# A router that works on blocks without 1/rms, and constants and position biases loaded in another order

## The chip, the cores and the metric

The kernel runs on one core of one Trainium2 chip. The metric is the time of one execution on the device in microseconds (us), the median of several runs. The program is one launch and computes everything in fp32. Its engines are TensorE (PE in the profile, with its weight loads PEld), VectorE (DVE), ScalarE (ACT), GpSimd (POOL) and SyncE (SP); each has its own stream of instructions, and they meet at semaphores.

## What is computed

Two blocks of a transformer follow one another on 256 tokens of width 1024. The change lies in the first. Cut to what matters:

```python
mod = jax.nn.silu(c) @ w_ada[l] + b_ada[l]                 # shifts, scales and gates, 6 x 1024
sh1, sc1, gt1, sh2, sc2, gt2 = jnp.split(mod[:, None, :], 6, axis=-1)
h = rms_norm(x, g_pre_mix[l]) * (1.0 + sc1) + sh1
proj = h @ w_in[l]                                         # 1024 x 3072
...                                                        # 4 differential heads, 8 neighbourhood heads
bias = rpb.astype(jnp.float32)[:, dr[:, None, :, None], dc[None, :, None, :]]   # position biases
mix = jnp.concatenate([o_diff, o_nat], axis=-1) @ w_out[l]
x = x + gt1 * rms_norm(mix, g_post_mix[l])
h2 = rms_norm(x, g_pre_ffn[l]) * (1.0 + sc2) + sh2
logits = (hf @ w_router + b_router).astype(jnp.float32)    # hf is h2, 256 x 1024; 32 experts
top_val, top_idx = lax.top_k(logits, TOP_K)                # 4 of 32, gates by softmax
...                                                        # each token through its 4 experts
```

## The kernel before

**Start.** SP loads `x` (L384), 8 chunks of `w_ada` and 12 chunks of `w_in` (L381, L373). ACT loads `c` (L1231), then the constants `early_sb` (L1232: identity, ones, masks, epsilons), then 14 small vectors. POOL waits for the eighth chunk of `w_ada`, then loads the distance biases (`alibi`, L450, 1 MB) and the neighbourhood biases (L460: 32 transfers of 64 x 4 rows of 64 numbers, 256 bytes each), then router weights and other small things. PE runs `turn_c` (L488), `turn_x` (L502), the chunks of `w_ada` (`ada`, L521) with `vector_columns` (L492 to L495, turning the small vectors) after the second and the squares' sum `sum_squares(0, q)` (L539) after the fourth, then `ada_columns(0)` (L531) and the twelve chunks of `w_in` (`win_half`, L642). DVE waits first for the turned vectors (L1589 to L1601), then makes 1/rms (L1559), multiplies x by it (L1616), copies the `w_ada` sum (L1606) and scales `hT`.

**Middle.** Attention is woven into 24 half chunks ("slots") of `w_in` and 4 slots of the other 16 chunks of `w_ada`. From slot 8 on PE flips one head's biases in each slot (`flip_bias`, L625), and DVE adds the window.

**Router.** After `w_out` (L562), ACT and DVE make 1/rms of its result (L1218, L1559), and `onto_x` (L1576, L1578) adds to x, a quarter at a time. ACT squares each quarter (L1209), PE sums the squares over all 128 partitions (L539), ACT takes the root, DVE the reciprocal (L1559), DVE multiplies x by it (L1698, 8 tiles), ACT scales and shifts into `hT` (L1304, 8 tiles). Then PE makes the logits (L707, L709 for the bias row) and turns `hT` into token rows (L713). DVE picks the top four (L1704 to L1714), PE counts ranks (L718 to L722), DVE lists the jobs (L1728 to L1741), PE turns the list (L725), then adds b2 (L735), gathers token columns for the first pair of experts (L741), and the expert loop begins (L776, then L805; the first 12 chunks of expert weights are loaded by then). The loop ran 34 jobs in the profiled execution. In it ACT copies the next pair's gathered columns out of PSUM with one instruction a job (`save_half`, L1318).

## Time and profile before

| | us |
|---|---|
| runs | 2051.84, 2049.17, 2051.05 |
| median | 2051.05 |
| profiled execution | 2057.52 |
| its span in the trace | 2055.7 |
| PE busy in the span | 1961.8 (95%) |
| mean granted share of TensorE's clock | 0.984 |

Times in the trace count from the start of the span. A line such as "PE ... x64" merges 64 instructions, with what they wrote and read; in brackets stands the idle time of the engine ahead of them and what ended it. The granted clock is 1.00 (2.4 GHz) or 0.50 (1.2 GHz); a number between is a mean over a stretch.

### The profile page before, as it was taken

How to read it: one execution, taken by the hardware profiler on the slowest of the kernel's cores; microseconds unless marked ns; L12 is line 12 of the kernel's file. 1: busy time of each engine (PE TensorE's matmuls, PEld its weight loads, DVE VectorE, ACT ScalarE, POOL GpSimd, SP SyncE). 2: the span in 40 equal slices, each digit the busy share in tenths (PEclk: the TensorE clock that was granted, in tenths of full speed). 3: DMA queues.
4: the chain of work that ended last, by engine and by line, in shares of the span. 5: the costliest groups of instructions: out<-in, count | busy, mean ns of one | idle time of the engine just before them, and what ended most of it. 6: DMA issues, size and time to landing. Idle time of an engine off the chain costs nothing.

```text
span 2055.7 us, 25409 instructions
## 1 busy us (share of the span) xinstructions
PE 1961.8 (95%) x10105; PEld 1256.3 (61%) x10106; DVE 461.2 (22%) x880; ACT 315.4 (15%) x585; POOL 28.3 (1%) x49
## 2 busy tenths in 40 slices
PE   6999699999999999999999989999999999999998
PEld 4776544433334444443333338788888899888887
DVE  1432411101111111111011113441010277410101
ACT  1232211101111111111011112431000120210001
POOL 4000000000000000000000000000000000000000
PEclk9999699999999999999999998999999999999999
DMA  9939199999997979999999996334444433344410
GB/s 325 306 105 401 62 393 421 422 422 422 422 422 315 422 317 423 422 422 422 422 421 422 422 383 212 103 103 143 151 157 146 143 121 103 124 143 146 162 41 21
DMA packets 170248, 562.81 MB, mean 274 GB/s; under 512 B 10726, under 2 KB 110216, under 8 KB 117712
## 3 DMA queue, kind: packets, MB, share of 16 engines
q1 hardware_dynamic: 167504, 554.83, 69.8%
q0 software_dynamic: 1920, 6.29, 1.1%
q8 instruction: 44, 0.72, 0.1%
q10 hardware_dynamic: 768, 0.87, 0.1%
q14 instruction: 12, 0.10, 0.0%
HBM read 560.91 MB, written 1.05 MB: 273 GB/s over the span
## 4 chain that ended last, share of the span: by engine, by line
PE 72%; DMA 20%; SPq 4%; DVE 1%; issue 1%; ACT 0%; DVEq 0%; ACTq 0%
DMA ring<-in_w_dram 18%; PE psum L1069 15%; PE psum L776 12%; PE psum L805 7%; PE psum L1041 7%; PE psum L1102 5%; PE psum L848 5%; SPq L401 3%; PE psum L642 3%; PE psum L562 3%; PE psum L741 2%; PE psum L757 2%; DMA ring<-in_w_in_dram 1%; PE psum L1123 1%; PE psum L539 1%
## 5 line engine op out<-in xcount | busy, mean ns | idle before, releaser
L776 PE MATMUL psum<-ring,arena 128*64 128x512 f32 x2176 | 491.4, 596 | 43.3 <-DMA ring<-in_w_dram 41.4
L776 PEld LDWEIGHTS psum<-ring,arena 128*64 128x64 f32 x2176 | 152.1, 137 | 376.2 <-issue 253.0
L1069 PE MATMUL psum<-hT,ring 128*128 128x256 f32 x1408 | 307.5, 379 | 0.0
L1069 PEld LDWEIGHTS psum<-hT,ring 128*128 128x128 f32 x1408 | 267.5, 190 | 36.4
L805 PE MATMUL psum<-ring,arena 128*64 128x512 f32 x1088 | 241.0, 595 | 3.3
L1798 DVE TENSOR_SCALAR arena<-psum 128x512 f32<-128x512 f32 x34 | 23.5, 692 | 736.8 <-PE psum L783 736.8
L805 PEld LDWEIGHTS psum<-ring,arena 128*64 128x64 f32 x1088 | 77.7, 137 | 144.7 <-issue 144.7
L1041 PE MATMUL psum<-arena,ring 128*128 128x256 f32 x640 | 141.4, 379 | 0.0
L1041 PEld LDWEIGHTS psum<-arena,ring 128*128 128x128 f32 x640 | 121.6, 190 | 16.5
L1329 ACT ACTIVATE arena<-arena 128x512 f32<-128x512 f32 x34 | 21.4, 630 | 515.4 <-DVE arena L1798 515.4
L741 PE MATMUL psum<-arena 128*128 128x128 f32 x576 | 81.0, 286 | 0.0
L1102 PE MATMUL psum<-hT,ring 128*128 128x256 f32 x352 | 79.1, 379 | 0.0
L741 PEld LDWEIGHTS psum<-arena 128*128 128x128 f32 x576 | 71.4, 196 | 11.9 <-issue 11.9
L1492 ACT ACTIVATE arena<-arena 128x512 f32<-128x512 f32 x22 | 13.9, 630 | 394.5 <-DVE arena L1939 394.5
L1102 PEld LDWEIGHTS psum<-hT,ring 128*128 128x128 f32 x352 | 65.8, 190 | 10.1 <-issue 1.9
L757 PEld LDWEIGHTS psum<-arena 64*128 64x128 f32 x560 | 51.2, 186 | 33.8 <-issue 27.6
L757 PE MATMUL psum<-arena 64*128 64x256 f32 x560 | 69.9, 389 | 0.7 <-ACT arena L1339 0.7
L1939 DVE TENSOR_TENSOR arena<-psum,rstd 128x512 f32<-128x512 f32 x22 | 15.2, 692 | 238.3 <-PE psum L1069 238.3
L848 PE MATMUL psum<-hT,ring 128*128 128x256 f32 x288 | 66.3, 384 | 0.0
L562 PE MATMUL psum<-mixT,ring 128*128 128x256 f32 x288 | 63.7, 379 | 0.0
L642 PE MATMUL psum<-hT,ring 128*128 128x256 f32 x256 | 60.1, 392 | 0.5 <-DVE hT L1622 0.5
L848 PEld LDWEIGHTS psum<-hT,ring 128*128 128x128 f32 x288 | 53.9, 191 | 9.3 <-issue 2.4
(346 smaller groups left out, 1602.8 us busy)
## 6 DMA issues: line engine op xcount, KB each, us to landing
ring<-in_w_dram SPq DMA_DIRECT2D x384, 1024.0 KB, 23.2
ring<-in_ffn_w_dram SPq DMA_DIRECT2D x66, 1024.0 KB, 5.2
ring<-in_w_ada_dram SPq DMA_DIRECT2D x24, 1024.0 KB, 10.8
ring<-in_odd_w_in_dram SPq DMA_DIRECT2D x16, 1024.0 KB, 5.4
ring<-in_even_w_in_dram SPq DMA_DIRECT2D x13, 1024.0 KB, 12.4
ring<-in_w_in_dram SPq DMA_DIRECT2D x12, 1024.0 KB, 14.2
ring<-in_w_out_dram SPq DMA_DIRECT2D x4, 1024.0 KB, 15.5
ring<-in_even_w_out_dram SPq DMA_DIRECT2D x4, 1024.0 KB, 5.1
```

What stands on the lines that cost most here:

```text
L401: sp.dma_start(home[:, :], src).then_inc(landed[(C_MOE + j) % RING], 16)
L562: mm = nc.tensor.matmul(home[:, at:at + n_out], lhs, rhs, start=(k == 0), stop=(k == KT - 1))
L642: mm = nc.tensor.matmul(home, lhs, rhs, start=(k == 0), stop=(k == KT - 1))
L741: nc.tensor.matmul(home[:, (k % 4) * P:(k % 4 + 1) * P], h_tok[:, a, k * P:(k + 1) * P], pick[:, a, :], start=(a == 0), stop=(a == TT - 1))
L757: mm = nc.tensor.matmul(bank[k // 2][:, (k % 2) * T:(k % 2 + 1) * T], y_sb[half, t * P:(t + 1) * P], st_sb[r][half, :], start=False, stop= ...
L776: mm = nc.tensor.matmul(bank[4 + q][64 * h:64 * h + 64, :], xg[:, k, SLOTS * r:SLOTS * (r + 1)], ring[(C_MOE + k) % RING][:, (2 * h + q) * ...
L805: mm = nc.tensor.matmul(bank[7][64 * h:64 * h + 64, :], act_T[:, at:at + 64], w[:, k, 512 * h:512 * h + 512], start=(f == 0), stop=(f == 7))
L848: mm = nc.tensor.matmul(home[:, at:at + n_out], lhs, rhs, start=(k == 0), stop=(k == KT - 1))
L1041: mm = nc.tensor.matmul(bank[j // 2][:, (j % 2) * T:(j % 2 + 1) * T], w[:, k, j * P:(j + 1) * P], ffn_h[i % 2][:, k, :], start=(i == 0 and ...
L1069: mm = nc.tensor.matmul(bank[4 + 2 * (i % 2) + b][:, h * T:(h + 1) * T], cols(n)[:, k, h * P:(h + 1) * P], hT[:, k * T:(k + 1) * T], start ...
L1102: mm = nc.tensor.matmul(home, lhs, rhs, start=(k == 0), stop=(k == KT - 1))
L1798: V.tensor_scalar(glu, both[:, :, 0], LIMIT, None, ALU.min).then_inc(S.glu_ready, 1)
```

## The change

Five edits.

1. **Constants.** `early_sb` is laid out anew. SP loads its first 258 columns (identity, ones, epsilons) ahead of `x`, with a semaphore of their own (`ident_loaded`); ACT loads the rest behind the 14 small vectors. PE waits for `early_loaded` only at the first flip, DVE at the first window.
2. **Position biases.** 16 transfers of 64 x 6 rows of 256 bytes instead of 32 of 64 x 4 rows. Each half of the partitions keeps six rows of windows, of which the two blocks of queries use overlapping four, so a flip is two matmuls of 256 columns instead of one of 512. POOL issues them when the third chunk of `w_in` has landed.
3. **Order on PE at the start.** The squares' sum after the second chunk of `w_ada`, the turned vectors after the sixth.
4. **Router.** logits = (x\*g)@w / rms + (shift@w + b). The row in brackets is made during `w_out` (8 matmuls of one column, one that spreads it). ACT scales x by the gain alone into `hT`, without waiting for 1/rms. PE takes each quarter as it comes (`routed_part`): column sums of the squares (`ones[:, 0:1]`, one output column), logits, and the turn into token rows. 1/rms is a number for each token (`tok_rstd`), applied by DVE to the logits and by ACT to the token rows.
5. **Gathered columns.** They now lack the shift, so `save_half` adds it: four instructions of 128 columns with a bias instead of one of 512 in each job; ahead of the loop ACT does one half and DVE the other.

```diff
-N_EARLY = _columns(EARLY, [("ident", P), ("ones", P), ("before", P), ("flip", P), ("slot", 2 * SLOTS), ("eps", 2),
+N_EARLY = _columns(EARLY, [("ident", P), ("ones", P), ("eps", 2), ("before", P), ("flip", P), ("slot", 2 * SLOTS),
...
+            first_part = EARLY["before"][0]
+            sp.dma_start(early_sb[:, 0:first_part], early[:, 0:first_part]).then_inc(S.ident_loaded, 16)
             sp.dma_start(x_tok, x[0].rearrange("(a p) d -> p a d", p=P)).then_inc(S.x_loaded, 16)
...
-            for r in range(GRID_ROWS):
-                half = 64 * (r % 2)
+            pool.wait_ge(landed[(C_WIN + 2) % RING], 16)
+            for half in range(2):
                 for h in range(8):
-                    src = bass.AP(nat_rpb.tensor, h * 465 + (NAT_KH - 1 - r) * 31 + NAT_KW - 1 - (GRID_W - 1),
-                                  [[1, GRID_W], [31, GRID_ROWS], [1, GRID_W]])
...
+                    src = bass.AP(nat_rpb.tensor, h * 465 + (NAT_KH - 3 - half) * 31 + NAT_KW - 1 - (GRID_W - 1),
+                                  [[1, GRID_W], [31, NAT_WINDOWS], [1, GRID_W]])
...
-            vector_columns()
-            for n in range(2, 4):
-                ada(n)
             for q in range(4):
                 sum_squares(0, q)
-            for n in range(4, N_ADA_A):
+            for n in range(2, 6):
+                ada(n)
+            vector_columns()
+            for n in range(6, N_ADA_A):
                 ada(n)
...
+                if j == 1:
+                    pe.wait_ge(S.mod_ready, 1)
+                    pe.wait_ge(S.moe_loaded, 16 * 5)
+                    for k in range(KT):
+                        mm = nc.tensor.matmul(bank[7][0:1, 0:E_N], mod[:, 24 + k:25 + k], router_w[:, k, :],
+                                              start=(k == 0), stop=(k == KT - 1))
+                    mm.then_inc(S.shift_turned, 1)
...
+            def routed_part(q):
+                pe.wait_ge(S.sq_ready, 4 * 2 + q + 1)
+                for k in (2 * q, 2 * q + 1):
+                    for a in range(TT):
+                        sums = nc.tensor.matmul(bank[5][:, a:a + 1], sq[:, k * T + a * P:k * T + (a + 1) * P], ones[:, 0:1],
...
+                for k in (2 * q, 2 * q + 1):
+                    pe.wait_ge(S.h_ready, KT + k + 1)
+                    for a in range(TT):
+                        block = hT[:, k * T + a * P:k * T + (a + 1) * P]
+                        mm = nc.tensor.matmul(bank[4][:, a * E_N:(a + 1) * E_N], block, router_w[:, k, :],
...
-            squares(xT, S.x_ready, 4)
-            root(2)
-            for k in range(KT):
-                act.wait_ge(S.spread, k + 1)
-                nc.scalar.activation(hT[:, k * T:(k + 1) * T], sq[:, k * T:(k + 1) * T], ACT.Identity,
-                                     bias=mod[:, 24 + k:25 + k], scale=pre_scale[:, 8 + k:9 + k]).then_inc(S.h_ready, 1)
-
+            for q in range(4):
+                act.wait_ge(S.x_ready, 4 + q + 1)
+                square(xT, q)
+                for k in (2 * q, 2 * q + 1):
+                    nc.scalar.activation(hT[:, k * T:(k + 1) * T], xT[:, k * T:(k + 1) * T], ACT.Copy,
+                                         scale=pre_scale[:, 8 + k:9 + k]).then_inc(S.h_ready, 1)
...
-            def save_half(home, dst):
-                nc.scalar.activation(dst, home.rearrange("p (k s) -> p k s", s=2 * SLOTS), ACT.Copy).then_inc(S.half_saved, 1)
+            def save_half(r, home, dst):
+                for k in range(4):
+                    ins = nc.scalar.activation(dst[:, k, :], home[:, k * P:(k + 1) * P], ACT.Identity,
+                                               bias=mod[:, 24 + 4 * r + k:25 + 4 * r + k])
+                ins.then_inc(S.half_saved, 1)
...
-            inverse(2)
-            for k in range(KT):
-                V.tensor_tensor(sq[:, k * T:(k + 1) * T], xT[:, k * T:(k + 1) * T], rstd[:, :], ALU.mult) \
-                 .then_inc(S.spread, 1)
```

The order of PE's matmuls at the start, before: `turn_c`, `turn_x`, then chunks of `w_ada` (written to 32 x 512), turned vectors, squares' sum (128x256), `ada_columns`, and the first chunks of `w_in`.

```order
L488 MATMUL psum<-early_sb,arena 128x8
L502 MATMUL psum<-early_sb,arena 128x128 x16
L521 MATMUL psum<-ring,small 32x512 x8
L492 MATMUL psum<-early_sb,arena 128x128
L493 MATMUL psum<-early_sb,arena 128x2
L495 MATMUL psum<-early_sb,arena 128x32 x2
L521 MATMUL psum<-ring,small 32x512 x8
L539 MATMUL psum<-sq,early_sb 128x256 x8
L521 MATMUL psum<-ring,small 32x512 x16
L531 MATMUL psum<-early_sb,arena 128x4 x4
L509 MATMUL psum<-small,early_sb 128x2
L642 MATMUL psum<-hT,ring 128x256 x32
```

And now:

```order
L492 MATMUL psum<-early_sb,arena 128x8
L506 MATMUL psum<-early_sb,arena 128x128 x16
L525 MATMUL psum<-ring,small 32x512 x8
L543 MATMUL psum<-sq,early_sb 128x256 x8
L525 MATMUL psum<-ring,small 32x512 x16
L496 MATMUL psum<-early_sb,arena 128x128
L497 MATMUL psum<-early_sb,arena 128x2
L499 MATMUL psum<-early_sb,arena 128x32 x2
L525 MATMUL psum<-ring,small 32x512 x8
L535 MATMUL psum<-early_sb,arena 128x4 x4
L513 MATMUL psum<-small,early_sb 128x2
L650 MATMUL psum<-hT,ring 128x256 x32
```

The sum of squares has moved up by one pair of chunks and the three rows of turned vectors down by four chunks.

PE from the third chunk of `w_out` (128x256 into `psum` from `mixT,ring`) to the counting of ranks, before:

```order
L562 MATMUL psum<-mixT,ring 128x256 x16
L539 MATMUL psum<-sq,early_sb 128x256 x12
L707 MATMUL psum<-arena,hT 128x32 x8
L709 MATMUL psum<-arena,early_sb 128x32
L707 MATMUL psum<-arena,hT 128x32 x8
L709 MATMUL psum<-arena,early_sb 128x32
L713 MATMUL psum<-early_sb,hT 128x128 x16
L718 MATMUL psum<-arena,early_sb 128x32
```

And now, from the matmuls of the shift on; the three rows of a quarter repeat four times:

```order
L710 MATMUL psum<-arena,small 1x32 x8
L566 MATMUL psum<-mixT,ring 128x256 x16
L543 MATMUL psum<-sq,early_sb 128x256 x2
L715 MATMUL psum<-arena,early_sb 128x32
L566 MATMUL psum<-mixT,ring 128x256 x16
L543 MATMUL psum<-sq,early_sb 128x256 x4
L723 MATMUL psum<-early_sb,sq 128x1 x4
L731 MATMUL psum<-arena,hT 128x32 x4
L737 MATMUL psum<-early_sb,hT 128x128 x4
L723 MATMUL psum<-early_sb,sq 128x1 x4
L731 MATMUL psum<-arena,hT 128x32 x4
L737 MATMUL psum<-early_sb,hT 128x128 x4
L723 MATMUL psum<-early_sb,sq 128x1 x4
```

The sums over 256 columns are gone, the logits and turns stand in quarters behind sums of one column, and eight matmuls of one row (`1x32`) and one that spreads it stand between the chunks of `w_out`.

ACT in the same place, from the last square of the `w_out` result on, before:

```order
L1209 ACTIVATE sq<-hT 128x512
L1218 ACT_TABLE_LOAD
L1218 ACTIVATE rstd<-psum,early_sb 128x256
L1209 ACTIVATE sq<-xT 128x512 x4
L1218 ACTIVATE rstd<-psum,early_sb 128x256
L1304 ACTIVATE hT<-sq,small 128x256 x8
L1310 ACT_TABLE_LOAD
L1310 ACTIVATE arena<-arena 128x32 x2
L1314 ACTIVATE arena<-psum 128x1024 x2
```

And now:

```order
L1237 ACTIVATE sq<-hT 128x512
L1246 ACT_TABLE_LOAD
L1246 ACTIVATE rstd<-psum,early_sb 128x256
L1237 ACTIVATE sq<-xT 128x512
L1333 ACTIVATE hT<-xT,small 128x256 x2
L1237 ACTIVATE sq<-xT 128x512
L1333 ACTIVATE hT<-xT,small 128x256 x2
L1237 ACTIVATE sq<-xT 128x512
```

The second root is no longer ahead of the copies into `hT`; each quarter's two copies follow its square.

## Rows read from the trace of the kernel before

**Rows 1.** The page, part 4: share of the span by line in the chain.
```profile
DMA ring<-in_w_dram 18%; PE psum L1069 15%; PE psum L776 12%; PE psum L805 7%; PE psum L1041 7%; PE psum L1102 5%; PE psum L848 5%; SPq L401 3%; PE psum L642 3%; PE psum L562 3%; PE psum L741 2%; PE psum L757 2%; DMA ring<-in_w_in_dram 1%; PE psum L1123 1%; PE psum L539 1%
```
**Rows 2.** The chain in order of time, first 420 us: start us, us, what.
```profile
83.68 3.45 PE psum L642 x16
...
398.28 26.88 DMA ring<-in_w_dram
```
**Rows 3.** Timeline of the start: start us, us, engine, line, instructions [idle before <-releaser].
```profile
20.26 0.47 PE L492 MATMUL psum<-early_sb,arena 128*128 128x128 f32 x1 [4.69 <-DMA arena<-in_cmp_pos_v_dram]
...
27.83 3.64 PE L521 MATMUL psum<-ring,small 128*32 128x512 f32 x32
...
33.30 1.41 PE L531 MATMUL psum<-early_sb,arena 128*128 128x4 f32 x8 [1.83 <-DVE arena L1606]
...
35.72 16.49 PE L642 MATMUL psum<-hT,ring 128*128 128x256 f32 x64 [0.50 <-DVE hT L1622]
...
54.47 8.77 PE L642 MATMUL psum<-ring,hT 128*128 128x256 f32 x32 [2.25 <-DMA ring<-in_w_in_dram]
```
**Rows 4.** The same timeline, DVE alone, from 20 to 36 us.
```profile
21.22 0.28 DVE L1589 COPY small<-psum 128x120 f32<-128x120 f32 x1 [20.10 <-PE psum L495]
...
22.26 0.07 DVE L1601 DVE_READ_ACCUMULATOR2_ANT small<- 1x1 f32 x1
28.44 1.75 DVE L1559 RECIPROCAL rstd<-rstd 128x256 f32<-128x256 f32 x1 [6.11 <-ACT rstd L1218]
30.23 2.29 DVE L1616 TENSOR_TENSOR sq<-xT,rstd 128x2048 f32<-128x2048 f32 x1
32.56 0.69 DVE L1606 COPY arena<-psum 128x512 f32<-128x512 f32 x1
```
**Rows 5.** The same timeline, POOL's transfers of the biases.
```profile
28.01 0.56 POOL L450 DMA_DIRECT2D early_sb<-in_early_dram  x1 [24.65 <-DMA ring<-in_w_ada_dram]
...
28.56 19.56 POOL L460 DMA_DIRECT2D arena<-in_nat_rpb_dram  x32
```
**Rows 6.** Stretches: us, busy us (instructions) by engine, PEclk, DMA share, GB/s.
```profile
36.00:54.00 18.00, 16.21 (x64) 13.52 (x63) 2.03 (x8) 1.20 (x2) 15.11 (x25) 0.87 1.08 217
58.00:78.00 20.00, 19.57 (x98) 16.09 (x97) 7.68 (x12) 5.47 (x18) 0.00 (x0) 1.00 1.10 349
211.00:214.60 3.60, 3.60 (x9) 2.84 (x10) 3.53 (x8) 1.26 (x2) 0.00 (x0) 0.50 0.58 244
223.50:235.20 11.70, 11.66 (x52) 11.41 (x53) 2.30 (x16) 1.82 (x3) 0.00 (x0) 0.50 0.00 0
262.00:396.00 134.00, 133.51 (x718) 56.42 (x716) 19.96 (x38) 17.09 (x29) 0.00 (x0) 1.00 1.01 420
```
**Rows 7.** Timeline of the router, 195 to 260 us.
```profile
210.97 5.69 PE L539 MATMUL psum<-sq,early_sb 128*128 128x256 f32 x16 [4.82 <-ACT sq L1209]
...
219.44 4.04 ACT L1304 ACTIVATE hT<-sq,small 128x256 f32<-128x256 f32 x8 [2.28 <-DVE sq L1698]
...
223.53 3.62 PE L707 MATMUL psum<-arena,hT 128*128 128x32 f32 x16 [6.88 <-ACT hT L1304]
...
231.88 0.21 DVE L1704 COPY arena<-psum 128x64 f32<-128x64 f32 x1 [10.13 <-issue]
...
233.14 0.20 DVE L1714 TENSOR_SCALAR arena<-arena 128x64 f32<-128x64 f32 x1
...
235.02 0.41 PEld L718 LDWEIGHTS psum<-arena,early_sb 128*128 128x128 f32 x2
...
236.51 0.18 DVE L1728 TENSOR_SCALAR arena<-psum 128x32 f32<-128x32 f32 x1 [2.00 <-issue]
...
256.14 4.08 PE L776 MATMUL psum<-ring,arena 128*64 128x512 f32 x18 [1.83 <-ACT small L1349]
```
**Rows 8.** A group of ACT in the expert loop, 262 to 396 us: count, busy us, mean ns.
```profile
L1318 ACT ACTIVATE arena<-psum 128x512 f32<-128x512 f32 x5 | 3.0, 597 | 0.3
```
**Rows 9.** Timeline of the expert loop, PE: second matrices of one job.
```profile
647.05 7.09 PE L805 MATMUL psum<-ring,arena 128*64 128x512 f32 x32
```

More of the change, by code:

```diff
@@ L621, in flip_bias @@
                 if h == 0:
-                    pe.wait_ge(S.bias_loaded, 16 * 32)
+                    pe.wait_ge(S.early_loaded, 16)
+                if h == 0:
+                    pe.wait_ge(S.bias_loaded, 16 * 16)
                 if h >= 2:
                     pe.wait_ge(S.bias_ready, h - 1)
-                nc.tensor.matmul(bank[(5, 7)[h % 2]], flip, nat_bias[:, h, :], start=True, stop=True) \
-                  .then_inc(S.bias_flipped, 1)
+                for n in range(2):
+                    mm = nc.tensor.matmul(bank[(5, 7)[h % 2]][:, n * T:(n + 1) * T], flip,
+                                          nat_bias[:, h, P * (1 - n):P * (1 - n) + T], start=True, stop=True)
+                mm.then_inc(S.bias_flipped, 1)
             def win_half(i, half):
@@ L710, in _ @@
-            mm.then_inc(S.logits_ready, 1)
-            for a in range(TT):
-                for k in range(KT):
-                    mm = nc.tensor.transpose(bank[2 * a + k // 4][:, (k % 4) * P:(k % 4 + 1) * P],
-                                             hT[:, k * T + a * P:k * T + (a + 1) * P], ident)
+                if j == 1:
[5 more added lines that the diff above has]
+                    mm.then_inc(S.shift_turned, 1)
@@ new lines, in _ @@
+                if j == 2:
+                    pe.wait_ge(S.shift_row_ready, 1)
+                    nc.tensor.matmul(bank[7][:, 64:64 + E_N], ones[0:1, :], shift_row, start=True, stop=True) \
+                      .then_inc(S.shift_spread, 1)
+            sum_squares(1, 3)
+            def routed_part(q):
[3 more added lines that the diff above has]
+                        sums = nc.tensor.matmul(bank[5][:, a:a + 1], sq[:, k * T + a * P:k * T + (a + 1) * P], ones[:, 0:1],
+                                                start=(k == 0 and a == 0), stop=(k == KT - 1), skip_group_check=True)
+                if q == 3:
+                    sums.then_inc(S.ssq_ready, 1)
+                for k in (2 * q, 2 * q + 1):
[3 more added lines that the diff above has]
+                        mm = nc.tensor.matmul(bank[4][:, a * E_N:(a + 1) * E_N], block, router_w[:, k, :],
+                                              start=(k == 0 and a == 0), stop=(k == KT - 1), skip_group_check=True)
+                if q == 3:
+                    mm.then_inc(S.logits_ready, 1)
+                for k in (2 * q, 2 * q + 1):
+                    for a in range(TT):
+                        mm = nc.tensor.transpose(bank[2 * a + k // 4][:, (k % 4) * P:(k % 4 + 1) * P],
+                                                 hT[:, k * T + a * P:k * T + (a + 1) * P], ident)
+                return mm
@@ L1243, in _ @@
                     act.dma_start(pos_rows[i][:, 64 * g:64 * g + 64], v[0]).then_inc(S.vec_loaded, 16)
+            act.dma_start(early_sb[:, EARLY["before"][0]:EARLY["alibi"][0]], early[:, EARLY["before"][0]:EARLY["alibi"][0]]) \
+               .then_inc(S.early_loaded, 16)
             act.wait_ge(S.c_cleared, 1)
@@ L1344, in _ @@
             act.wait_ge(S.gathered, 1)
-            for r in range(2):
-                save_half(bank[6 + r], xg[:, 4 * r:4 * r + 4, :])
+            save_half(0, bank[6], xg[:, 0:4, :])
             save_gates(0, bank[5])
```

50 lines of the change are left out of this document (31 added, 19 removed).

## The prediction

> **What bounds the kernel now.** First the page's list of the chain by line: 18% is waiting for expert weights, nearly all the rest is PE [rows 1]. The chain in order of time shows the pattern: PE's steps follow one another without a gap until PE waits 26.88 us for expert weights, from 398.28 us on [rows 2]. From 262 to 396 us the DMA engines already move 420 GB/s with PE busy 133.5 of 134 us [rows 6], so in the expert loop the stream of weights is the limit. That stream starts when PE has used up its first chunk, in the row that begins at 256.14 us [rows 7]. What moves this row moves the stream, the loop and all behind it by as much; so the question is when that row begins. Two stretches ahead of it hold idle time that a reader can see.
>
> The first is the start. PE turns the small vectors at 20.26 us, after 4.69 us of waiting. It is done with the last chunk of `w_ada` at 31.47 us, though POOL's wait shows this chunk landed at 28.01 us [rows 3, 5]. DVE is the later one: 1/rms and the product occupy it from 28.44 to 32.52 us, and only then it copies the `w_ada` sum [rows 4]. The chunks of `w_in` begin at 35.72 us; the third of them is waited for 2.25 us, and the row behind that wait is slow, 8.77 us for what takes 2 x 3.45 at full clock [rows 2, 3].
>
> The second is the router: one step after another on ACT, PE and DVE, with PE at a granted clock of 0.50 from 223.5 to 235.2 us [rows 6, 7].
>
> **The start, edits 1 to 3.** The last chunk of `w_ada` is bound by the transfers: the bytes ahead of it stay nearly the same, so it still lands near 28.0 us. PE then takes 0.9 us for it (3.64 / 4), or 1.8 at half clock, and ends at 28.9 to 29.8. But DVE's program begins with the turned vectors, and these now come after the sixth chunk. That one lands two chunks of 2.5 us (1 MB at 420 GB/s) ahead of the last, at 23.0. PE needs 0.9 to 1.8 us for it and 1.0 to turn the vectors (20.26 to 21.22), so DVE starts at 24.9 to 25.8. It needs 1.1 us for the small work, 1.8 for 1/rms and 2.3 for the product [rows 3, 4], and copies the sum at 30.1 to 31.0, not at 32.56. DVE stays the later one. From that copy to the first matmul of `w_in` it took 3.16 us; if PE is at half clock all the while, its eight instructions there (1.41 us, partly at full clock) take some 0.4 more. I take the first matmul at 33.4, a gain of 2.3 us (1.2 to 3.0). The earlier identity and x gain nothing by themselves, since the chunks cover them.
>
> Now the wait for the third chunk. From 36 to 54 us the engines of the DMA were fully busy but moved 217 GB/s, against 349 from 58 to 78 us [rows 6]. So 3.9 MB went through in 18 us, of which 2.1 MB were biases in pieces of 256 bytes. The other 1.8 MB need 5.2 us at 349 GB/s, which leaves 12.8 us for the biases. With 1.57 MB instead it is 9.6 us. They now stand behind the third chunk: three chunks and the 1 MB of `alibi` are 4.2 MB, 12.0 us, all landed by 40.0. The second chunk is wanted at 33.4 + 6.9 + 2.5 (half clock at first, as before) = 42.8, the third at 49.7, the fourth at 56.6. Even if every bias went ahead of the fourth chunk, that one would land at 40.0 + 9.6 + 3.0 = 52.6. So the wait goes, and with it the slow row behind it: 2.25 us and 8.77 - 6.90 = 1.87 us. Next late would be the biases themselves at the first flip, which comes after four chunks, later than 61 us. POOL issues 16 transfers in 10 us (0.61 each [rows 5]), up to 50. Before, it had issued the last at 48.1 us and the third chunk, clogged by them, was in at 54.5; allowing the same 6.4 us they are there by 57. The split flips stream the same columns. Between the first slots and the router PE has no idle worth naming, so the 6.4 us (2.3 + 2.25 + 1.87) are kept. Bounds: 4.8 (late start, half clock a little longer) to 9 (first chunks at full clock).
>
> **The shift's row, edit 4.** Eight matmuls of one column and one that spreads the row are 18 instructions on PE in the midst of `w_out`, where PE has no gap: a cost. The nearest row is the logits, 16 instructions in 3.62 us at half clock, 0.226 each [rows 7], so 0.113 at full clock and 2.0 us in all. Those load 128 columns of weights and not one, so it may be less; bounds 0.8 and 2.5, and I take 1.7. DVE's two small instructions for it lie under `w_out`.
>
> **The router, edit 4.** PE starts on the first square as before, at 210.97. A quarter is now 8 instructions of column sums, 8 of logits, 4 turns; all four are 80. At half clock each is 0.226 (from 223.5 to 235.2 us 52 took 11.66 [rows 6]), so they end at 210.97 + 18.1 = 229.1, the last logits four instructions earlier, at 228.2. PE's sums over four quarters ended 5.69 us after the first began, so DVE and ACT give a quarter every 1.5 us at most; ACT now has 2 x 0.505 for two tiles (8 in 4.04 [rows 7]) on top of a square of some 0.6 us, 1.6 us a quarter against PE's 4.5, so PE is the bound. The second root, DVE's second 1/rms and its eight products leave the chain. DVE had the logits at 231.88; now at 228.3. It needs 1.46 us to the end of L1714 and 0.2 more for a second instruction: masks at 229.95, when the turns are done. Before, the masks were there at 233.34 but PE began to count at 235.02, behind the turns. Its ten instructions took 1.5 us; now, without the full clock that the turns had brought, 2.3. DVE goes on at 232.5, not at 236.51 [rows 7]: 4.0 us gained, bounds 2.5 and 6. What follows, 19.6 us up to 256.14, is unchanged; the first pair's columns are saved by ACT and DVE side by side in place of two instructions of ACT, which I put at nothing.
>
> **The clock in the router.** This is the term I am least sure of. In the trace PE was busy from 223.5 to 235.2 us and was granted 0.50 throughout, with outputs of 32 and then 128 columns; from 211.0 to 214.6, with 256 columns, it was 0.50 too [rows 6]. The new quarters, with 1, 32 and 128 columns, are nearest to the first of these. The Trainium skill, TensorE: Matmul & The Clock Gate, section "What's actually happening", says that sustained activity releases the throttle. By that the quarters would end at full clock, which is the first rival; the trace of the logits speaks against it.
>
> **The expert loop, edit 5.** ACT has four instructions instead of one of 0.597 us [rows 8]. Bounds for four: 0.6 (same columns) and 2.4; I take 1.2, so 0.6 more a job. ACT is busy 17.09 us in five jobs, 3.4 a job, and this copy comes while PE does the second matrices, 7.09 us [rows 9]; the rest that ACT does there is under 2 us. Hidden, cost 0; without this cover it would cost 0.6 us for each of some 34 jobs. The Trainium skill, ScalarE: Activation LUTs, section "What ACT_TABLE_LOAD costs", gives 280 ns and 0.833 ns a column with a bias from memory, and an overlap of 93 ns: by it four take some 1.3 us, an estimate; no row of this trace shows such an instruction.
>
> **Sum.** 6.4 - 1.7 + 4.0 = 8.7 us. The profiled execution would go from 2057.5 to 2048.8. It lay 6.5 us above the median of the runs, a distance I assume unchanged; so the median goes from 2051.05 to 2042.3.
>
> **Rivals.** (a) *Full clock in the router.* If it is granted after the first quarter, PE takes 4.5 + 3 x 2.3 = 11.4 us for 80 instructions instead of 18.1, and the count 1 us less: 7.7 more, 2034.6. For it speaks that PE is busy without a break, against it the logits of before. (b) *The small matmuls cost more at half clock*, 0.27 each by changes of kind and waits at quarters; 80 of them eat the 4.0 us: 2046.3. Against it: rows of alternating kinds already keep 0.22. (c) *The edit of the biases doesn't do what it says*: they still hold back the third or fourth chunk, or are late at the flip, and the 4.1 us of wait and slow clock come back in another place: 2046.4. For it: pieces of 256 bytes clog the engines as before. (d) *Slower.* In the loop ACT's four instructions delay what the next job waits for. It decides when ACT's work between the gather and the end of the second matrices passes 7.09 us; I count under 3. If it did, 34 x 0.6 = 20 us would come on top: 2062.7.
>
> **Chances.** Forecast 0.63 (own range 2038.5 to 2045.5), (a) 0.15, (b) 0.10, (c) 0.08, (d) 0.04. A measurement of this kernel can tell about 0.2% (4.1 us) from no change, so faster means below 2047.0. The forecast and (a) are surely there, (b) and (c) lie at the edge and give 0.10 of their 0.18: faster 0.88, same 0.08, slower 0.04. The range 2034.0 to 2046.5 takes in (a) and the better halves of (b) and (c) and leaves out under 2 in 10.
>
> **What would show it.** In the new trace: the first matmul of `w_in` at 32.7 to 34.5; no wait of PE on `w_in` and one slow stretch fewer; no wait at the first flip; 18 instructions in 0.8 to 2.5 us in `w_out`; from the first column sum to the last turn 18 us at clock 0.50; DVE's rank step some 21.5 us after the first column sum (25.5 before); the first expert matmul near 247.4. It would be wrong if the chunks of `w_ada` ended later, if PE waited at a flip, if the clock rose in the quarters, or if the expert loop's jobs took longer than 26.6 us where PE sets the pace.

## The result and the profile after

| | before | after |
|---|---|---|
| runs | 13 | 13 |
| median, us | 2052.08 | 2049.01 |
| lowest to highest, us | 2048.31 to 2054.96 | 2043.17 to 2052.84 |
| profiled execution, us | 2057.52 | 2047.21 |
| its span, us | 2055.7 | 2045.1 |
| mean granted clock | 0.984 | 0.984 |

The ratio of after to before is 0.998, with a 95% interval from 0.9971 to 0.9989: 2.3 to 6.0 us faster, at the edge of the 0.2%, where 8.7 us were forecast. The profiled executions lie 10.3 us apart, the medians 3.1. The larger part of this document is about that difference. A run more than 1.5% above the fastest of the same kernel is left out of every median here and below: one of 2934.44 us (edit 2 alone) and, among the cut kernels, one of 273.96 (14 fillers), 258.83 and 259.28 (router), and 265.56, 265.75 and 266.0 (one more transfer).

The timeline of the start, PE alone (start us, us, engine, line, instructions, idle before and its releaser), for [rows 3]:

```profile
28.39 1.94 PE L525 MATMUL psum<-ring,small 128*32 128x512 f32 x8 [0.42 <-DMA ring<-in_w_ada_dram]
32.02 1.87 PE L535 MATMUL psum<-early_sb,arena 128*128 128x4 f32 x8 [1.69 <-DVE arena L1639]
...
34.90 16.26 PE L650 MATMUL psum<-hT,ring 128*128 128x256 f32 x64 [0.50 <-DVE hT L1655]
50.99 7.07 PE L650 MATMUL psum<-ring,hT 128*128 128x256 f32 x32
```

The same stretch on DVE, for [rows 4]:

```profile
27.17 1.74 DVE L1592 RECIPROCAL rstd<-rstd 128x256 f32<-128x256 f32 x1
28.94 2.29 DVE L1649 TENSOR_TENSOR sq<-xT,rstd 128x2048 f32<-128x2048 f32 x1
31.27 0.69 DVE L1639 COPY arena<-psum 128x512 f32<-128x512 f32 x1
```

And POOL's position biases, for [rows 5]:

```profile
40.95 10.35 POOL L464 DMA_DIRECT2D arena<-in_nat_rpb_dram  x16 [11.77 <-DMA ring<-in_w_in_dram]
```

DVE's 1/rms and product now end at 31.2 us, not 32.5, and PE begins with `w_in` at 34.90, not 35.72. POOL issues 16 transfers from 40.95 us on. The third chunk of `w_in` is there when PE wants it: the row at 50.99 has no wait and its 32 instructions take 7.07 us. All three are what the change was meant to do. The last chunk of `w_ada` itself was 0.6 us later than before: POOL's wait for it ended at 28.63 us, where it had been 28.01 [rows 5].

The chain in order of time in `w_out` and the router, for [rows 7]:

```profile
183.86 0.56 PE psum L710 x16
...
192.39 0.33 PE psum L715 x2
...
207.12 1.87 PE psum L723 x8
208.99 1.76 PE psum L731 x8
210.74 0.91 PE psum L737 x4
...
219.97 1.50 PE psum L723 x8
221.47 1.77 PE psum L731 x8
...
227.45 0.37 DVE arena L1767 x3
...
232.26 7.19 PE psum L763 x16
239.45 6.04 PE psum L769 x32
...
245.74 1.14 ACT arena L1350 x4
...
247.62 13.96 PE psum L804 x64
```

The shift's row costs 0.56 + 0.33 = 0.89 us. Column sums (L723), logits (L731) and turns (L737) follow one another without a gap. DVE goes on with the ranks at 227.45, 20.3 us after the first column sum; before it was 25.5 [rows 7]. The first expert matmul stands at 247.62 us, 8.5 us earlier than at 256.14.

Not all of the 10.3 us between the two profiled executions is the change. From the last expert matmul of the first block to the end of the span the trace of before took 836.0 us and that of after 832.9, in code that the change doesn't touch. In the first 60 us of that stretch the granted clock was 0.89 before and 0.97 after. In the eleven traces of full kernels of this document the stretch takes from 832.9 to 836.3 us, with either start and either router, so some 3 us of the distance are luck.

Stretches of after (us, busy us and instructions by engine, granted clock, DMA share, GB/s), for [rows 6]:

```profile
36.00:54.00 18.00, 18.00 (x77) 15.51 (x76) 1.08 (x5) 1.19 (x2) 13.05 (x21) 0.91 1.09 285
58.00:78.00 20.00, 19.57 (x100) 16.37 (x100) 10.61 (x17) 6.96 (x22) 0.00 (x0) 1.00 1.10 339
206.60:223.50 16.90, 16.38 (x79) 16.38 (x80) 4.60 (x13) 7.10 (x14) 0.00 (x0) 0.50 0.08 34
```

From 36 to 54 us the engines of the DMA now move 285 GB/s where they moved 217. In the quarters of the router PE is busy 16.38 of 16.90 us and is granted 0.50 throughout.

The group of ACT's copies in the expert loop, 262 to 396 us (count, busy us, mean ns), for [rows 8]:

```profile
L1350 ACT ACTIVATE arena<-psum,small 128x128 f32<-128x128 f32 x20 | 5.7, 368 | 0.3
```

Four of them take 5.7 / 5 = 1.14 us a job, where one took 0.60.

### The profile page after: what moved, and what is told of

Its sections match the earlier page's. It is cut to its first block, busy times and chain, and to the rows that moved or that the text cites. A ratio compares the mean times of both kernels' runs of the same rounds, so it can differ in the third digit from the quotient of the medians.

```text
span 2045.1 us, 25591 instructions
## 1 busy us (share of the span) xinstructions
PE 1963.2 (96%) x10151; PEld 1258.7 (62%) x10152; DVE 457.9 (22%) x877; ACT 332.7 (16%) x689; POOL 19.1 (1%) x33
## 4 chain that ended last, share of the span: by engine, by line
PE 78%; DMA 15%; SPq 4%; DVE 2%; issue 1%; ACT 0%; DVEq 0%; ACTq 0%
PE psum L1097 15%; DMA ring<-in_w_dram 14%; PE psum L804 14%; PE psum L833 8%; PE psum L1069 7%; PE psum L1130 5%; PE psum L876 5%; SPq L405 4%; PE psum L650 4%; PE psum L566 3%; PE psum L769 3%; PE psum L785 2%; PE psum L1151 1%; PE psum L811 1%; PE psum L543 1%; DMA ring<-in_w_ada_dram 1%
```

## Experiments

**Terms.** "The old biases" are 32 transfers issued as soon as the eighth chunk of `w_ada` is in, "the new biases" edit 2. A cut kernel does all up to the gather for the first experts, waits for the first expert chunks, writes the token rows and stops: the expert loop and everything behind it are left out. It ends after some 255 us, and with some five runs each, which lie within 2.5 us, it tells differences of about one microsecond in the first part. Edits 1 and 3 were not tried apart from each other.

### The full kernel, before and in parts

Four full kernels: before again, after again, before with edits 1 to 3 (start), before with edits 4 and 5 (router). All share 31 runs of before, with a median of 2053.55 us (2048.35 to 2057.18).

> The kernel before, unchanged, for a second trace and five more rounds beside the parts. The profiled execution of before (2057.5 us) lay 6.5 us above the median, that of after (2047.2) 1.8 us below its own; between the two traces the first expert matmul moved by 8.5 us, yet the medians differ by 3.1. Theory A (the traces were lucky and unlucky): another trace of before is shorter, 2048 to 2054 us of span, and its first expert matmul begins earlier than 256.1 us, or its granted clock behind the loop is better. Theory B (the gain is real up to the first expert matmul and lost in or behind the expert loop in most executions): the first expert matmul begins again at 255 to 257 us.

> The changed kernel, unchanged, for a second trace and five rounds. Ratio 0.998 as before. Theory A: the first expert matmul lies where it lay, 247.6 us, within 3 us; the spread of 2043 to 2053 us comes from the granted clock. Theory B: it lies at 247.6 and the stretch from there to the end is longer than the 1797.5 us of the first trace by 3 us or more.

> Only edits 1 to 3 (constants, biases, order on PE at the start); the router is that of before. By the prediction's sum 6.4 us faster, ratio 0.9969. If the wait for the third chunk is not there in most executions of before: 2 to 3 us, ratio 0.9988.

> Only edits 4 and 5 (router on blocks without 1/rms, shift added to the gathered columns); the start is that of before. By the prediction's sum 4.0 - 1.7 = 2.3 us faster, ratio 0.9989; by the price of the shift's row in the trace of after (0.56 + 0.33 us) it would be 3.1 us, 0.9985. If edit 5 costs time in the expert loop: no change or slower.

| kernel | runs | median | ratio to before, 95% | first expert matmul in the trace |
|---|---|---|---|---|
| before again | 12 | 2054.79 | 1.0003 (0.9993 to 1.0013) | 254.8 |
| after again | 9 | 2049.3 | 0.9974 (0.9963 to 0.9984) | 248.2 |
| start, edits 1 to 3 | 12 | 2050.63 | 0.9986 (0.9976 to 0.9996) | 249.9 |
| router, edits 4 and 5 | 11 | 2049.63 | 0.998 (0.9971 to 0.9988) | 252.5 |

After again is 3.3 to 7.6 us faster, in line with the first comparison. The start by itself gives 2.9 us (0.8 to 4.9), against 6.4 forecast. The router by itself gives 4.1 us (2.5 to 6.0); forecast was 4.0 - 1.7 = 2.3. So the term that fell short is in the start. The stretch from the first expert matmul to the end of the span took 1799.1 us in before again and 1799.5 in after again (1799.6 and 1797.5 in the first two traces), so the missing gain isn't lost there.

### The first part alone

The cut in short, with the same lines on PE, ACT, DVE and POOL (a return ahead of the loop):

```diff
             sp.wait_ge(S.count_ready, 1)
+            for j in range(PER_EXPERT):
+                sp.wait_ge(landed[(C_MOE + j) % RING], 16 * ((C_MOE + j) // RING + 1))
...
+            for a in range(TT):
+                sp.dma_start(out[0, a * P:(a + 1) * P, :], h_tok[:, a, :]).then_inc(S.out_stored, 16)
+            sp.wait_ge(S.out_stored, 16 * TT)
+            return
             with sp.Fori(0, E_N - 1) as e:
```

> The kernel before, cut off where the expert loop would begin: the first pair's columns and gates are gathered and saved, the token rows of the router are stored as the output, and everything from the first expert on is left out. It measures by itself, over many executions, the time up to the first expert matmul, which in the two traces of before was 256.1 and 254.8 us. Theory A (the traces stand for all executions): 258 to 268 us with the stores. Theory C (in most executions this part is shorter than in the traces, by the clock or the wait for the third chunk): less, and the difference to the cut kernel after is 3 to 5 us.

> The changed kernel with the same cut. Theory A: 7.5 us less than the cut kernel before (traces: 247.6 and 248.2 against 256.1 and 254.8), so the whole gain is made here in every execution, and what is missing in the full kernels' medians (about 4.8 us of gain) is lost behind the first expert matmul. Theory C: 3 to 5 us less.

> Edits 1 to 3 alone with the same cut. By the traces (249.9 us against a mean of 255.5) 5.5 us less than the cut kernel before; by the prediction 6.4; by the full kernels' medians 2.9.

> Edits 4 and 5 alone with the same cut. By the traces (252.5 against 255.5 us) 3.0 us less than the cut kernel before; by the prediction 2.3. It does not run the expert loop, so if the full kernel with these edits alone gains less than this one, edit 5 costs time in the loop.

| cut kernel | runs | median (lowest to highest) | against cut before | full median minus cut median |
|---|---|---|---|---|
| before | 5 | 258.28 (257.5 to 259.39) | | 1795.3 |
| after | 5 | 253.31 (251.47 to 253.81) | -5.0 | 1796.0 |
| start | 5 | 256.1 (255.08 to 257.26) | -2.2 | 1794.5 |
| router | 4 | 254.96 (253.82 to 256.34) | -3.3 | 1794.7 |

The parts add up within the spread of the runs: 2.2 + 3.3 = 5.5, and 5.0 together. (Over all six runs of the router the median is 255.65, 2.6 less than cut before.) The last column takes the full medians of the table above. It is 1794.5 to 1796.0 for all four, so no more than some 2 us of what is won in the first part can be lost in or behind the expert loop. The traces are finer here: from its first to its last expert matmul the loop took 961.8 to 963.6 us in the six full kernels with one copy of ACT a job and 963.2 to 964.6 us in the five with four. The means are 962.7 and 963.9 us, so the four copies may cost about a microsecond in all.

And cut before, unlike the full kernel, doesn't wait for its third chunk in its trace. PE in the trace of cut before:

```profile
36.43 15.61 PE L653 MATMUL psum<-hT,ring 128*128 128x256 f32 x64 [0.80 <-DVE hT L1635]
51.88 7.07 PE L653 MATMUL psum<-ring,hT 128*128 128x256 f32 x32
```

With the same 32 transfers ahead of it the chunk had landed 51.1 us into the trace; PE wanted it at 51.9. The margin is under a microsecond. In the full kernels with the old biases it landed between 54.2 and 55.4 us. The order of arrival differs with it: in the full kernels with the old biases the third chunk landed 0.4 to 1.2 us behind the last bias, in cut before and the cut router 2.4 and 2.1 us ahead of it. So by these seven traces the stall of 2.25 us in [rows 3] hangs on which transfers arrive first.

### How often the stall is there

Before twice more, for one trace each, and before with edit 2 alone:

```diff
-            for r in range(GRID_ROWS):
-                half = 64 * (r % 2)
+            pool.wait_ge(landed[(C_WIN + 2) % RING], 16)
+            for half in range(2):
...
-                                  [[1, GRID_W], [31, GRID_ROWS], [1, GRID_W]])
+                                  [[1, GRID_W], [31, NAT_WINDOWS], [1, GRID_W]])
...
-                nc.tensor.matmul(bank[(5, 7)[h % 2]], flip, nat_bias[:, h, :], start=True, stop=True) \
-                  .then_inc(S.bias_flipped, 1)
+                for n in range(2):
+                    mm = nc.tensor.matmul(bank[(5, 7)[h % 2]][:, n * T:(n + 1) * T], flip,
+                                          nat_bias[:, h, P * (1 - n):P * (1 - n) + T], start=True, stop=True)
+                mm.then_inc(S.bias_flipped, 1)
```

> One more trace of the kernel before. In the three traces of full kernels with its start PE waited 2.2 to 2.7 us for the third chunk of w_in (landed at 54.2 to 54.5 us); in the two cut ones not at all (51.1 and 51.3 us). If the wait belongs to some executions only: absent here or in the next one. If it belongs to every execution of the full program: 2.2 to 2.7 us again in both.

> A further trace of the kernel before, for the same question: if the wait of 2.2 to 2.7 us for the third chunk belongs to some executions only, it is absent here or in the trace ahead of this one; if it belongs to every execution of the full program, it is in both.

> Edit 2 alone: 16 transfers of biases behind the third chunk of w_in, flips split; constants, order on PE and router as before. It takes away the wait for the third chunk and the slow row behind it and nothing else. If every execution of before has them: 4.1 us faster, ratio 0.998. If few have them: under 1 us, no difference that can be measured.

The row of the third chunk on PE's timeline in four traces. The first of these views ends at 62 us; the whole row of 32 instructions takes 10.24 us.

Before, first of the two:

```profile
55.40 6.78 PE L642 MATMUL psum<-ring,hT 128*128 128x256 f32 x16 [3.17 <-DMA ring<-in_w_in_dram]
```

Before, second of the two:

```profile
54.60 7.17 PE L642 MATMUL psum<-ring,hT 128*128 128x256 f32 x32 [2.56 <-DMA ring<-in_w_in_dram]
```

Before again, of the first set:

```profile
54.55 7.17 PE L642 MATMUL psum<-ring,hT 128*128 128x256 f32 x32 [2.65 <-DMA ring<-in_w_in_dram]
```

Edit 2 alone:

```profile
52.15 7.07 PE L647 MATMUL psum<-ring,hT 128*128 128x256 f32 x32
```

The stall is in all five traces of full kernels with the old biases (2.2 to 3.2 us). The half clock behind it is missing in two of the three rows of before shown here: 7.17 us for 32 instructions is close to the 7.07 at full clock, and the granted clock in the last of them is 1.00. With edit 2 alone the stall is gone, the chunk landed at 40.9 us, and the first expert matmul stands at 252.2, against 256.1, 254.8, 259.6 and 254.9 in the four traces of before: 2.6 to 7.4 us earlier, 4.1 in the mean, as forecast. But the time: 2051.96 us, the median of 11 runs (2049.02 to 2054.14), a ratio of 0.9994 (0.9985 to 1.0003) to before, whose 17 runs have a median of 2053.52. That is 1.6 us faster by the medians, 1.2 by the ratio and 3.1 at the most, where 4.1 were forecast; no gain at all lies within the interval too.

The traces are of the first execution of a kernel in its set, the medians mostly of later ones (the first trace of before, 2057.52 us, stands beside its set). Such first or traced executions of before were 2057.52, 2055.72, 2056.33, 2052.95, 2056.80, 2056.15, 2058.00, 2057.87 and 2052.98 us, on average 2056.0, over medians between 2051.8 and 2054.8. Of the kernel with edits 4 and 5, which keeps the old biases, the first one was 2053.60, 4.0 over its median. Of the kernels with the new biases the first ones were 2047.21, 2049.58, 2050.48 and 2052.85, over medians of 2049.01, 2049.3, 2050.63 and 2051.96: nearly level. So what edit 2 takes away seems to sit mostly in first executions. Two of the nine of before are not above the median, and the one of 2052.95 us had a stall of 2.56 us all the same: the stretch behind its expert loop took 833.9 us, some 2 less than in the two longer traces of before with 836.0, and made up for most of it.

Does a late third chunk cost its full length where it is surely late? Cut before with one more transfer of 1 MB on POOL's queue ahead of the 32:

```diff
+            pool.dma_start(mixT[:, :], early[:, EARLY["alibi"][0]:]).then_inc(S.more_loaded, 16)
             for r in range(GRID_ROWS):
```

> The kernel before, cut off ahead of the expert loop, with one more transfer of 1 MB on POOL (the distance biases once more, into a buffer that is not used yet) ahead of the position biases. In the cut kernel before the third chunk of w_in landed at 51.1 us, 1 us ahead of need; this transfer should delay it by some 3 us, to 54, as in the traces of the full kernels. If timed executions behave as traced ones: the trace shows 2 to 3 us of wait and a half-clock row, and the median rises by 3.5 to 4.5 us, to about 262. If the wait is there only or mostly while a trace is taken: the trace shows it, and the median rises by under 2 us.

Three of its six runs took 260.99 to 262.79 us, 261.64 in the median, 3.4 more than cut before. The other three took 265.56 to 266.0, and the trace is of one of these. In it the third chunk landed at 56.6 us:

```profile
56.69 9.48 PE L654 MATMUL psum<-ring,hT 128*128 128x256 f32 x32 [4.33 <-DMA ring<-in_w_in_dram]
```

A wait of 4.33 us and a row that is 2.4 us too long make 6.7 us; the span is some 8 us longer than that of cut before (263.8 and 255.9 us). The quickest of the six runs lies above the longest of cut before, 259.39. So a stall there is not hidden by anything. The quicker three, with a mean granted clock of 0.906 to 0.913 against 0.901 in the longer ones, may have had the wait without the row at half clock; no trace of them tells. What was wrong in the forecast is then not what the stall costs, but how often it is there.

### The clock in the router

In after, PE's quarters stayed at 0.50 with PE all but fully busy. Ahead of them stands an idle stretch of 4.82 us, then come three smaller ones (0.9, 2.2 and 0.7 us). If these hold the clock down, matmuls without a use in them should bring it back. Cut after, with 14 matmuls (28 instructions) into a bank that nobody reads:

```diff
             sum_squares(1, 3)
+            for n in range(14):
+                nc.tensor.matmul(bank[3][:, 0:256], ones, mixT[:, 0:T], start=True, stop=True)
```

> The changed kernel, cut off ahead of the expert loop, with 14 matmuls of 256 columns added on PE behind the last sum of squares of the w_out result (into a bank that is written again later). They fill the 5.8 us in which PE waits for x and in which its granted clock fell to 0.50. If the idle time is what keeps the router's quarters at half clock: the quarters start at clock 1.00 and take 8 to 12 us instead of 16.2, so 4 to 8 us less than the cut changed kernel (253.3). If the quarters lower the clock by themselves: at most 3 us less, the clock falls within them.

It took 248.07 us, the median of 5 (247.8 to 248.86), 5.2 less than cut after. PE in its trace:

```profile
200.28 6.21 PE L730 MATMUL psum<-mixT,early_sb 128*128 128x256 f32 x28
206.32 0.95 PE L736 MATMUL psum<-early_sb,sq 128*128 128x1 f32 x8
207.13 1.06 PE L744 MATMUL psum<-arena,hT 128*128 128x32 f32 x8
208.02 0.64 PE L750 MATMUL psum<-early_sb,hT 128*128 128x128 f32 x4
...
214.26 1.71 PE L736 MATMUL psum<-early_sb,sq 128*128 128x1 f32 x8
215.83 1.90 PE L744 MATMUL psum<-arena,hT 128*128 128x32 f32 x8
217.54 1.09 PE L750 MATMUL psum<-early_sb,hT 128*128 128x128 f32 x4
```

The first two quarters run at full clock, 2.2 us each and not 4.2. The fillers themselves overrun the gap: the column sums begin 7.0 us after the start of the last sum of squares of the `w_out` result, and 5.95 without fillers. From the last sum of squares that overlaps `w_out` to the gather the trace shows 36.1 us, 3.6 less than after. Another 1.4 us lie ahead of the fillers, in code that is the same as in cut after, and I can't say why; so 3.6 us are what this trace shows for the fillers. At 211.3 us the clock fell to 0.50 in the midst of the quarters. That speaks against the Trainium skill, TensorE: Matmul & The Clock Gate, section "What's actually happening", read as a rule for this place: it has activity release the throttle, and here PE had instructions without a break. No trace here tells whether the small output, or something else about these instructions, is the reason.

Two more steps: seven further fillers of the same form, in which `fill(n)` stands for n matmuls (one ahead of the count of ranks, four behind it, two ahead of b2), and DVE's 1/rms and product ahead of its small work at the start.

```diff
+            fill(4)
             pe.wait_ge(S.jobs_listed, 1)
...
+            fill(2)
             pe.wait_ge(S.gates_saved, 1)
```
```diff
+            inverse(0)
+            link(V.tensor_tensor(tiles(sq[:, :]), tiles(xT[:, :]), bcast(rstd[:, :], KT), ALU.mult))
             dve.wait_ge(S.vec_turned, 1)
...
-            inverse(0)
-            link(V.tensor_tensor(tiles(sq[:, :]), tiles(xT[:, :]), bcast(rstd[:, :], KT), ALU.mult))
             save_ada(0)
```

> c_warm (248.15 us) with seven more filling matmuls of 256 columns in PE's later gaps: one behind the top four, four behind the ranks, two behind the turned gates. If idle gaps hold the clock down to the gather: up to 5 us less than c_warm, since b2's matmuls and the gather run at clock 1.00. If b2's matmuls (32 rows of weights) and the small ones keep it down by themselves: the same as c_warm or up to 3 us more, the price of seven matmuls at half clock.

> c_warm with DVE's 1/rms and product of the start moved ahead of its work on the turned vectors. In the trace of the changed kernel DVE began 1/rms at 27.17 us, behind those vectors, and copied the w_ada sum at 31.27, though PE had it at 30.32. With the new order DVE is ready at 22 us and PE's last w_ada chunk decides: 1.0 us less, or up to 2 where that chunk runs at full clock.

The seven fillers: 243.32 us (243.16 to 243.96, 5 runs), 4.8 less again. DVE's order: 247.29 (246.79 to 248.69, 5 runs), 0.8 less than without it, which is within the spread of these two sets of runs. The traces don't show the microsecond that was expected: DVE copies the `w_ada` sum at 29.53 us, and at 29.68 without the new order. Then the full kernels, after with the 14 fillers, and after with all three:

> The changed kernel, whole, with the 14 filling matmuls ahead of the router's quarters. The cut form gained 5.2 us over the cut changed kernel (248.15 against 253.31), so the full kernel's median should be 5 us below that of the changed one: about 2044, ratio to before 0.9953.

> The full kernel after, with the 14 filler matmuls behind the sum of squares of w_out, the seven later ones in the gaps of the router (one, four and two, 128x256 each), and DVE's 1/rms and product ahead of the small vectors at the start. If what the cut kernels gained adds up: the kernel with 14 fillers alone had 2044.2; less 4.8 for the later fillers and 0.9 for DVE's order gives 2038.5, a ratio to before of 0.993; first expert matmul at about 237 us. If the clock given back in the router is lost again in or behind the expert loop, the ratio stays near 0.9954 (2044).

The first had 2044.19 us (2041.92 to 2044.83, 5 runs), a ratio of 0.9954 (0.9941 to 0.9967) to before. The second had 2037.52 us (2035.98 to 2039.79, 6 runs), beside 2053.62 for before (11 runs): a ratio of 0.992 (0.9907 to 0.9932). It beats both kernels. PE in its trace:

```profile
199.53 1.03 PE L543 MATMUL psum<-sq,early_sb 128*128 128x256 f32 x4
...
202.01 6.21 PE L719 MATMUL psum<-mixT,early_sb 128*128 128x256 f32 x28
208.05 0.95 PE L725 MATMUL psum<-early_sb,sq 128*128 128x1 f32 x8
...
223.21 3.76 PE L749 MATMUL psum<-mixT,early_sb 128*128 128x256 f32 x8
226.90 0.87 PE L762 MATMUL psum<-early_sb,arena 128*1 128x128 f32 x6
...
229.01 3.72 PE L773 MATMUL psum<-arena 32*128 32x256 f32 x16
232.66 3.84 PE L779 MATMUL psum<-arena 128*128 128x128 f32 x32
...
238.59 11.81 PE L814 MATMUL psum<-ring,arena 128*64 128x512 f32 x54 [1.88 <-ACT small L1392]
```

From the last sum of squares under `w_out` to the first expert matmul it is 39.1 us; in after it was 48.0 (from 199.66 to 247.62). b2 takes 3.72 us and not 7.19, the gather 3.84 and not 6.11. The first expert matmul stands 9.0 us earlier and the end of the span 8.0 us (2037.1 against 2045.1): the gain goes through to the end. DVE's order can't be seen in this trace: DVE was free of 1/rms and product at 22.3 us, but PE began the last chunk of `w_ada` only at 29.05 us, 0.7 later than in after, and took 1.93 us for it at half clock as there. So DVE copied the sum at 31.05, after PE and not after its own work, 0.2 us earlier than in after.

## Why the prediction was wrong, point by point

The direction was right. The time was not: 2042.3 was forecast, 2034.0 to 2046.5 as the range, and 2049.01 came out, 2.5 us above its end. A microsecond of this is the starting point: the three runs of before that the forecast built on had a median of 2051.05, the thirteen beside after 2052.08.

**What bounds the kernel: right.** The first expert matmul moved and the end moved with it. All four pairs of full and cut medians say so, and the last experiment does with 9.0 us in the trace.

**The first matmul of `w_in`, 2.3 us: within its bounds, in the traces nearer the lower one.** The cut kernels give 2.2 us for edits 1 to 3, and the trace of cut before has no stall to lose. In the trace of after the row begins at 34.90, where 32.7 to 34.5 was forecast, and at 34.3 in after again. Over all traces of full kernels it begins at 35.3 to 36.6 us with the old start and at 34.1 to 34.9 with the new one, 1.6 us earlier in the mean. In after DVE's chain ran as counted, from a start at 26.14 that was 0.3 us behind the later bound. So was its copy at 31.27, and from that copy to the first matmul it took 3.63 us, where 3.16 and the 0.4 for half clock were counted.

**The wait for the third chunk and the slow row, 4.1 us: the step that failed.** The mechanism was right. The old biases do hold the third chunk back (it landed at 54.4 us with them and at 40.9 with edit 2 alone), and a stall there is not hidden (at least 3.4 us in the runs of the test, 6.7 in its trace). The size was read off one execution: in the medians edit 2 is worth 1.2 to 1.6 us (3.1 at the most), not 4.1. The step that let this through was "It lay 6.5 us above the median of the runs, a distance I assume unchanged". An execution that lies 6.5 us above the median holds something that the median one does not, and a wait on a transfer with a margin of 1 to 3 us is the first candidate. The distance did not stay: the traced execution of after lay 1.8 us below its median. By the rows, 1.87 us of the 4.1 hung on the clock besides, and two of three further traces of before had the wait without it. (The 1.87 is 0.2 too high in itself: 8.77 is a row of the timeline, where 32 instructions at full clock take 7.07, and 2 x 3.45 comes from the chain.) Without the 4.1 us the same sum would have been 2.3 - 1.7 + 4.0 = 4.6 us and 2046.4.

What stays open: no trace of a later execution is at hand. That the stall is mostly absent in those is worked out from medians: from edit 2 alone, and from the full kernels with the old biases, which lie no further above their cut ones (1795.3, 1794.7) than those with the new biases (1796.0, 1794.5), though the cut ones of before and of the router had no stall in their traces. One trace of before had the stall in an execution of 2052.95 us, which is a median time, though with a short stretch behind the loop. And being the first execution can't be the whole reason, since the traces of the two cut kernels with the old biases are of first executions too and had the chunk in time. Why every traced full kernel lost the race and neither of these cut ones did is not settled.

**The shift's row, 1.7 us: 0.9.** I had priced it from matmuls with 128 columns of weights, with the bound of 0.8 for weights of one column; it lay by that bound. 16 such instructions take 0.56 us.

**The router, 4.0 us: low by about 1.** Quarters of 4.2 us and not 4.5 behind the first: column sums take 0.19 us each, not 0.226. The last logits ended 16.1 us after the first column sum (207.12 to 223.24), where 17.2 were forecast. The rank step came 20.3 us after the first column sum; 21.5 was forecast. That gives 5.2 us. (The forecast's own terms, 229.95 + 2.3, make 232.25 and not 232.5.) Two rows of the chain of before, which were not shown ahead, belong to what follows:

```profile
248.51 5.59 PE psum L741 x32
...
254.35 1.09 ACT arena L1318 x2
```

Of the 5.2 us 0.4 went back into the gather (6.04 us and not 5.59). Saving the first columns costs nothing, as said: 1.14 us against 1.09. With the shift's row the net is 3.9 us in the trace, 3.3 by the cut medians and 4.1 (2.5 to 6.0) by the full ones; 2.3 was forecast.

**The clock.** It stayed at 0.50 through the quarters, as the forecast had it and against rival (a). With fillers the first expert matmul came 9.0 us earlier, more than rival (a)'s 7.7, but not in the place that (a) names: 5.7 of the 9.0 are b2 and the gather (3.72 and 3.84 us, not 7.19 and 6.11), and the quarters still fell to half clock on the way.

**The expert loop, nothing: right, to about a microsecond.** 1.14 us for four instructions where 1.2 was estimated, a price of 0.54 us a job, hidden: 34 times that would be 18 us, and the difference of full and cut medians has no room for more than 2; the traces show some 1.2. By the figures of the Trainium skill, ScalarE: Activation LUTs, section "What ACT_TABLE_LOAD costs", one such instruction takes 387 ns, an estimate (280 + 0.833 x 128). The trace has 368.

**Rivals.** The times of (b) and (c), 2046.3 and 2046.4, were the nearest, but not their reasons: the small matmuls were cheaper than counted, and the biases were in time. (d) did not happen.

## What to carry to other kernels

A wait that one traced execution shows is a sample. Where it hangs on which of two transfers comes first, with a margin as small as the wait, and where that execution lies above the median by about as much, take its gain at a fraction and put the rest into the range. The rest of a long kernel can differ by luck between two traces as well, here by 3 us behind the loop; so compare the stretch that the change touches. A kernel cut off behind the part in question shows differences of about one microsecond where the full one of 2050 us shows two, and the difference of full and cut tells whether the gain survives. In a chain of short steps on several engines look for the idle stretches of TensorE ahead of rows at half clock, and fill them with matmuls nobody reads: here 21 of them, with two instructions moved on DVE, brought 11.5 us (2049.01 to 2037.52), three to four times what the change itself brought to the median.

## What the runs showed of the hardware

A filler may delay the work behind it and still win: 28 instructions overran their gap by 1.1 us and gave back 5 in the medians, 3.6 of them visible in the trace. The clock fell to 0.50 at 211.3 us in the midst of matmuls with 1, 32 and 128 output columns, without a gap on PE. Eight matmul instructions of one output column with 128 columns of weights take 0.95 us at full clock and 1.71 to 1.87 at half by their rows, 0.81 and 1.57 to 1.73 to the start of the next row, so some 0.10 and 0.20 us each. One with a single column of weights and 32 output columns takes 0.035 us at a granted clock of 1.00 (16 in 0.56). And the biases in 16 transfers and not 32, behind the third chunk, raised what the DMA engines move between 36 and 54 us from 217 to 285 GB/s (288 with edit 2 alone).
